# One named table set for logarithm and exponential on ScalarE, loaded at the head of each stage

## What is computed

```python
def rmsnorm(x, w):
    x32 = x.astype(jnp.float32)
    y = x32 * lax.rsqrt(jnp.mean(x32 * x32, axis=-1, keepdims=True) + RMS_EPS)
    return (y * w.astype(jnp.float32)).astype(x.dtype)
...
    kk = heads(k * p['rwkv_k_k'][j])
    kk = kk / jnp.maximum(jnp.sqrt(jnp.sum(kk * kk, axis=-1, keepdims=True)), 1e-12)
...
    var = jnp.mean(jnp.square(y - mu), axis=-1, keepdims=True)
    y = ((y - mu) * lax.rsqrt(var + GN_EPS)).reshape(b, s, D_INNER)
```

## Time and profile before

| what | value |
|---|---|
| median of 3 runs | 4746.25 us (4737.63, 4746.25, 4748.11) |
| profiled execution | 4737.78 us |
| its span, first to last instruction | 4735.7 us |
| PE busy | 4270.4 us, 90% |
| DVE busy | 2681.0 us, 57% |
| ACT busy | 2037.1 us, 43% |
| DMA, mean | 102 GB/s |

### The profile page before, as it was taken

One profiled execution on the slowest core, in us unless ns is written; L12 is line 12 of the kernel. 1 busy time (PEld: TensorE's weight loads), 2 busy tenths in 40 slices (PEclk: granted clock), 3 DMA queues, 4 the chain that ended last, 5 costly groups with the idle time before them and its releaser, 6 DMA issues. The chain is left out here.

```text
span 4735.7 us, 137117 instructions
## 1 busy us (share of the span) xinstructions
PE 4270.4 (90%) x60992; PEld 3646.6 (77%) x60992; DVE 2681.0 (57%) x4653; ACT 2037.1 (43%) x3614; POOL 4.6 (0%) x10
## 2 busy tenths in 40 slices
PE   6999979999996899999998999889999799999968
PEld 2888768888884889766667999868888688888848
DVE  5432557777774644355556433466325577787745
ACT  5432224555555652355556000175422255555453
POOL 0000000000000000000000000000000000000000
PEclk8999989999998999899999999989999899999989
DMA  7444773332325132100000222113437733333241
GB/s 296 147 124 126 208 227 86 96 97 82 97 70 187 63 83 55 51 1 1 1 15 23 98 90 71 62 42 100 121 117 213 238 88 97 85 94 97 70 178 63
DMA packets 542153, 480.74 MB, mean 102 GB/s; under 512 B 29312, under 2 KB 500608, under 8 KB 533632
## 3 DMA queue, kind: packets, MB, share of 16 engines
q1 hardware_dynamic: 410752, 405.91, 27.1%
q10 hardware_dynamic: 130816, 66.07, 5.1%
HBM read 337.94 MB, written 128.71 MB: 99 GB/s over the span
## 5 line engine op out<-in xcount | busy, mean ns | idle before, releaser
L633 PE MATMUL ps<-big_r,stage_r 128*128 128x384 f32 x2976 | 643.2, 351 | 18.0 <-DVE big_r L883 16.7
L633 PEld LDWEIGHTS ps<-big_r,stage_r 128*128 128x128 f32 x2976 | 524.3, 190 | 102.4 <-issue 56.8
L2461 PE MATMUL ps<-big_r,w_out 128*128 128x384 f32 x2304 | 417.3, 341 | 39.3 <-DVE w_out L2577 39.0
L2461 PEld LDWEIGHTS ps<-big_r,w_out 128*128 128x128 f32 x2304 | 406.5, 191 | 48.4 <-DVE w_out L2577 42.1
L633 PE MATMUL ps<-big_r,w_slab_r 128*128 128x384 f32 x1488 | 340.8, 336 | 0.0
L367 PE MATMUL ps<-big_r,stage_r 128*128 128x384 f32 x1536 | 311.5, 337 | 15.1 <-DVE big_r L354 15.0
L2185 DVE TENSOR_REDUCE extra<-ps 128x1 f32<-128x1152 f32 (+1 forms) x144 | 177.7, 1234 | 205.1 <-PE ps L2092 205.1
L367 PEld LDWEIGHTS ps<-big_r,stage_r 128*128 128x128 f32 x1536 | 270.4, 189 | 30.1 <-issue 28.3
L1448 ACT COPY arena<-ps 128x512 f32<-128x512 f32 x288 | 168.9, 587 | 254.6 <-PE ps L1253 254.1
L633 PEld LDWEIGHTS ps<-big_r,w_slab_r 128*128 128x128 f32 x1488 | 268.5, 189 | 0.0
L1602 DVE COPY_PREDICATED arena<-arena,ps 128x128 f32<-128x128 uint32 x720 | 192.8, 324 | 111.1 <-PE ps L1241 110.0
(11 more groups left out here) (259 smaller groups left out, 8191.9 us busy)
## 6 DMA issues: line engine op xcount, KB each, us to landing
w_slab<-in_w SPq DMA_DIRECT2D x138, 512.0 KB, 3.6
scan_in<-x_resid ACTq DMA_DIRECT2D x112, 576.0 KB, 5.9
arena<-scan_in SPq DMA_DIRECT2D x144, 320.0 KB, 3.8
arena<-scan_in SPq DMA_DIRECT2D x288, 128.0 KB, 3.8
arena<-scan_in SPq DMA_DIRECT2D x48, 576.0 KB, 7.6
arena<-scan_in SPq DMA_DIRECT2D x144, 192.0 KB, 3.9
arena<-in_w_ada SPq DMA_DIRECT2D x24, 1024.0 KB, 6.0
x_resid<-in_w_ada SPq DMA_DIRECT2D x24, 1024.0 KB, 4.9
```

Source lines behind the costliest of these rows:

```text
L633: mm = pe.matmul(g.ps[:, 3 * s + c, 0:CW], w[:, k * P:(k + 1) * P], x[:, k, chunk(c)], start=k == i == 0, stop=k == NB - 1 and i == 2)
L2461: mm = pe.matmul(g.ps[:, bank(i, b), 0:wide[i]], w[:, b, k * P:(k + 1) * P], r, start=k == j == 0, stop=k == NB - 1 and j == 2)
```

## The change

Six kinds of places get a named load, act.preload_act_table_set: of the set natural_log_exp_and_others (LN_EXP), which has both Ln and Exp, of exp_and_others for the tanh, and of sigmoid_and_others. Where a named set is active that has the function, no load is placed before it. With the sigmoid loads that are still placed by the compiler in the RWKV and the attention projections, there are 14 table loads instead of 136. Nothing else is changed.

```diff
@@ constants
+LN_EXP, EXP_TANH, SIGMOID = "natural_log_exp_and_others", "exp_and_others", "sigmoid_and_others"
@@ phase_open
         def _(act):
+            act.preload_act_table_set(SIGMOID)
             act.wait_ge(cond_in, 16)
             nc.scalar.activation(sig, cond, ACT.Sigmoid).then_inc(sig_ok, 1)
+            act.preload_act_table_set(LN_EXP)
             for b in range(NB):
@@ phase_rwkv_project
+            act.preload_act_table_set(EXP_TANH)
             A.copy(strided(xx[:, 0, :], 0, (T, NB), (CTX, 2)), strided(h[:, 0, :], 1, (T, NB), (CTX, 2))).then_inc(edge_ok, 1)
```

## The result

| | before | after |
|---|---|---|
| median of the timed runs | 4742.02 us (4737.63 to 4748.11, 4 runs) | 4701.74 us (4697.31 to 4703.43, 4 runs) |
| the profiled execution's own time, its span | 4737.78, 4735.7 us | 4700.37, 4698.6 us |
| table loads | 136 | 14 |

The ratio is 0.9913, with a 95% interval of 0.9896 to 0.9930: faster by 0.9%, 40.3 us between the medians. The forecast was 4700, in a range of 4686 to 4716, with 44.3 us gained.

A forecast was written before the change was run, and what follows sets the result against it. PE was taken as busy almost throughout, except in finish stages, where ACT with its loads had no slack. Gains 30.8 + 4.8 + 1.3 + 2.6 + 1.3 + 3.5 = 44.3 us gave 4693.5 or 4702; 4700 taken, range 4686 to 4716.

The forecast's parts named there:

- Finish stages: Two finish stages: block period falls from 7.32 to 6.07 us, bound by PE; 15.4 us gained each, 30.8 together.
- built alike: Two finish stages: the 15.4 us worked out for the first counts for the second too, 30.8 in all.
- ACT has no slack in it: Finish block: ACT's work with both loads and small gaps fills the whole 7.3 us period; without loads about 4.8.
- Boundaries: Boundary tails: second root's loads uncovered, 1.6 us each for three, 4.8; at the last, first root's Exp load, 1.3.
- Scans: Scan heads: the load moved to the head hides in ACT's idle time; 1.3 us each, 2.6 in all.
- rival 2: Projection and stage-head gains are swallowed later, such as by stores ACT awaits before a sigmoid: 4706 us; chance 0.12.
- Opening: Opening: the load between Ln and Exp is on the path, with DVE waiting for Exp; 1.3 us gained.
- Projection: RWKV projection: 1.3 at the receptance turn, 1.06 later, 2.3 per layer; tanh load loses 1.1 in layer 3; net 3.5.
- Rival 1: Finish stages give 2.5 to 5.5 us less each, from PE's clock falling or third product waiting longer: 4705 to 4711; chance 0.2.
- Rival 3: Granted clock falls for the whole finish stage because PE works in short bursts: 4799 us; chance 0.015.
- Rival 4: Automatic placement still puts its own sets before Ln and Exp, named loads only add: 4746 to 4752 us; chance 0.025.
- Rival 5: A load also drains the engine, costing twice its row; some eleven serial loads give another 1.28 each: 4686 us; chance 0.03.

The follow-up runs named there:

- the first pair: The first profile of the kernel before and of the changed kernel, both unchanged; the profiled executions took 4737.78 and 4700.37 us.

## Why the prediction held, point by point

**Finish stages: mechanism right, 28.8 to 28.9 us instead of 30.8.** Three terms were off. First, the new period is 6.16, not 6.07: the ring that sets it is the first variance product, 0.85 to Ln (1478.57 to 1479.42), 0.58, 0.15 to the third product, then 0.72 to the first centering product and 3.87 to the next variance, 6.17. The prediction took 0.645 for the 0.72, though rows 4 show it (1499.72 to 1500.44): a product behind a wait is followed 0.07 later than one in a stream. With 0.02 on the result that is the difference, 0.4 us a stage. Second, "built alike" was wrong for what is removed: the third block's Exp, where the clock fall sits, came 9.50 behind the second's in the first stage and 8.37 in the second, 8.0 to 9.5 in the six stages of three profiles. The first stage, from which the sum was made, was the dear one. Third, the first variance product starts 14.2 to 15.8 us behind the stage's start in the six profiles of the two kernels, which in the first pair cost 0.3 in the first stage and gave 0.4 in the second.

**"ACT has no slack in it" was the wrong reason for a right number.** The sum of ACT's work made 7.3 because the exponential's load had filled idle time that reappears when it goes. With both loads this sum is a ring too, as long as the one through PE; without the exponential's load that one still stands at 7.32, and without the logarithm's neither does. The load between Ln and Exp could have stayed at a period of 6.16. Of the two loads only the one ahead of Ln was on the path of a block; the other cost 1.3 us ahead of the first Exp and 1.3 in the step to the second, in each stage (51.7 us from the first variance product to the end against 49.1). The prediction would have priced a change that removes only the exponential's loads at 1.28 a block, some 20 us in all; the stages of the two experiments with one load a block say 5 to 6.

**Boundaries.** 1.4 to 1.7 in the first pair, 1.6 predicted, and 1.28 at the last, 1.3 predicted. The third boundary gave 0.8 in three profiles against three (139.65 to 138.84 us); the first pair had 1.5, and over all kernels, by whether they have the old loads there (4 profiles) or the new ones (10), it is 1.3.

**Scans.** Seen at the head as predicted, and lost in a spread that was not foreseen. That is part of rival 2, and not shown to be either swallowed or kept.

**Opening.** The load's 1.3 us are gone from DVE's wait: 2.42 in place of 3.71. But the DVE operation ahead of the root started at 33.94 instead of 33.17 in this execution, so the stage shows 0.5; three profiles against three have 0.35. Over all kernels it is 0.8 (55.4 us in the 4 profiles with the old loads, 54.6 in the 10 with the new). The stage's length moves by 1.7 us among those ten, so the term is read at its place, where it is 1.29.

**Projection: both terms right, what reaches the end open.** In layer 3 the first combination is 1.05 later, and up to the first rates three profiles of each kernel agree. DVE meets an earlier root in every key block, 1.27 to 1.28 us, from the first one on:

```profile
3249.81 1.42 DVE L894 SCALAR_TENSOR_TENSOR x_resid<-x_resid,chan 128x1152 f32<-128x1152 f32 x1 [3.71 <-ACT x_resid L731]
```

```profile
3227.16 1.42 DVE L899 SCALAR_TENSOR_TENSOR x_resid<-x_resid,chan 128x1152 f32<-128x1152 f32 x1 [2.44 <-ACT x_resid L734]
```

But it then waits for PE again (1.22 us before its next maximum, L894, where it had no wait), and PE stays 1.05 behind: before the turn the gain hides, as predicted. PE itself gains at two places, the turn to receptance and the first rates. Before, then after:

```profile
3324.80 1.56 PE L660 MATMUL ps<-x_resid,head_ones 128*128 128x384 f32 x4 [0.77 <-ACT x_resid L725]
...
3333.99 0.91 PE L660 MATMUL ps<-x_resid,head_ones 128*128 128x384 f32 x2 [1.38 <-DVE x_resid L889]
...
3374.75 0.92 PE L669 MATMUL ps<-x_resid 64*128 64x384 f32 x4 [1.05 <-ACT x_resid L747]
```

```profile
3302.50 1.45 PE L663 MATMUL ps<-x_resid,head_ones 128*128 128x384 f32 x4
...
3311.34 0.91 PE L663 MATMUL ps<-x_resid,head_ones 128*128 128x384 f32 x2 [1.14 <-DVE x_resid L894]
...
3350.99 0.92 PE L672 MATMUL ps<-x_resid 64*128 64x384 f32 x4
```

Counted from the starts of the stage (3176.61 and 3154.19), PE is 1.05 behind until the first row, 0.23 ahead at the second and 1.34 at the third: 1.28 gained at the turn (1.3 predicted) and 1.11 at the first rates (1.06 predicted). In layer 0 the same two places give 1.31 and 1.11 in the first pair. What of it reaches the end is open within the spread: 1.6 us in layer 3 by three profiles (1.2 predicted); over all kernels, those with the old loads have 569.1 us (4 profiles) and those with the new ones 567.9 (8). Layer 0 gained 3.9 (2.3 predicted), and the surplus lies ahead of the roots: behind the products of the conditioning vector (L166), where the prediction has no gain, PE is 1.2, 2.3 and 0.9 us ahead in the three pairs of profiles. These products wait for weights that come by DMA, 21.2 to 23.4 us in all before and 18.9 to 20.5 after; why less is not shown.

**The rivals.** Rival 1 was right in direction, the finish stages giving about 1 us less each, short of its 2.5: the period is 0.09 longer than forecast, and the clock does not fall. Rival 2 is open: the wait for a store that it names is there, and what it swallows is within the spread. Rival 3 fell: the clock is 1.00 behind the head. Rival 4 fell with the count of 14 loads. Rival 5 fell with the 1.27 to 1.41 us that a load gone or moved gave where somebody waited for it. That the forecast of 4700 came as near as it did (4701.74) is in part luck, since two errors met: 4 us less was gained than the sum said, and the kernel before ran at 4742.0 instead of the 4746.25 from which it was taken.

## What to carry to other kernels

A table load, or any fixed cost of an engine, is priced by its place, not by the engine's sum of work: look for idle time of that engine behind it before the next thing that others wait for. A sum of an engine's work that equals the period is no proof that the engine sets it; follow the ring of dependences through all engines, and name its members with the cost of a restart behind each wait. An engine that comes earlier at one place keeps nothing of it if it next waits for another engine: count a gain on the engine that sets the pace, at the rows where it stops waiting. And where a stage's length moves by more between two profiles of the same kernel than the term in question, read the term at its place, and not off the stage's end.

## What the runs showed of the hardware

A load for the set that is already there takes 1.28 us like any other, in three places; ahead of Ln it has 0.02 us on either side. PE's product behind a wait is followed 0.72 us later, where a stream has 0.645. The scan stages, on one core, last 781.2 to 794.8 us over all profiles, with the same instructions but for the place of one load; their mean granted clock is 0.977 to 0.986. After a wait of 3.48 us of PE the granted clock was 0.62 over a stretch of 9 us in one finish stage (rows 5, 6) and 0.72 over one of 6 us in the other, which had the same wait. With the load behind Exp, PE waits 2.20 us at this place in both finish stages; in the first the granted clock was 0.83 over the 10 us around it, and products behind it start up to 1.29 apart, in the second they start 0.645 apart. Rows of the kernel before, its timeline of PE and its busy time by stretch (columns of rows 1):

```profile
4552.14 1.52 PE L1784 MATMUL ps<-stage,head_ones 128*128 128x384 f32 x2 [3.48 <-ACT arena L1812]
```

```profile
4551.00:4557.00 6.00, 4.86 (x10) 2.83 (x11) 3.79 (x5) 4.72 (x7) 0.00 (x0) 0.72 0.38 117
```
